# Halving the last down weights of each layer by columns, and issuing an even and an odd head's value products together

## What is computed

```python
for i in range(seq // BLOCK_Q):               # 128 queries at a time
    p = softmax(where(mask, q_i @ k[:q1].T * scale + bias, -inf))
    o_i = p @ v[:q1]                          # the value products
...
x = layer_norm(DN_ALPHA * x + mixer(x), *ln1)
x = layer_norm(DN_ALPHA * x + moe(x), *ln2)
...
def expert_step(acc, p):                      # over 64 experts
    wg, wu, wd, g = p                         # 1024x256, 1024x256, 256x1024
    hid = silu(t @ wg) * (t @ wu)
    return acc + (hid @ wd) * g[:, None], None
```

## Time and profile before

| what | value |
|---|---|
| median of 3 runs | 1332.64 us (1332.28 to 1334.15) |
| profiled execution | 1336.95 us |
| its span, first to last instruction | 1335.1 us |
| mean granted TensorE clock | 0.922 of full speed |
| PE busy | 1096.8 us (82%) |
| weight loads on PE | 658.8 us |
| VectorE busy | 414.9 us (31%) |
| ScalarE busy | 260.8 us (20%) |
| main DMA queue | 439.25 MB, 80.4% of the 16 engines' span |
| chain that ended last | PE 56%, DMA 35%, issue 3%, VectorE 2% |

### The profile page before, as it was taken

The page is one execution under the profiler, slowest core; times in us unless marked ns, Lnnn a source line. Parts: engine busy times, 40 slices in busy tenths (PEclk is TensorE's granted clock), DMA queues, the critical chain, the costliest instruction groups (busy, mean ns, idle before and its releaser), DMA issues.

```text
span 1335.1 us, 19927 instructions
## 1 busy us (share of the span) xinstructions
PE 1096.8 (82%) x7616; PEld 658.8 (49%) x7616; DVE 414.9 (31%) x993; ACT 260.8 (20%) x619; POOL 79.9 (6%) x106
## 2 busy tenths in 40 slices
PE   6988999999777766766599999999997776776664
PEld 4764754544444434433288866545544444333331
DVE  2584533332212222111322235433322122221113
ACT  3463322221111111111023223222111111111110
POOL 0443100000000000000240000000000000000000
PEclk9988899999988888888799999999999888888886
DMA  8172469999999999999951163599999999999993
GB/s 341 59 283 94 174 252 393 415 416 417 374 421 422 421 423 421 423 422 421 359 193 64 64 252 126 236 392 415 418 418 371 420 422 421 423 421 423 421 421 135
DMA packets 75745, 447.52 MB, mean 335 GB/s; under 512 B 7451, under 2 KB 20183, under 8 KB 25510
## 3 DMA queue, kind: packets, MB, share of 16 engines
q1 hardware_dynamic: 72640, 439.25, 80.4%
q0 software_dynamic: 1904, 6.46, 1.4%
q10 hardware_dynamic: 1142, 1.01, 0.2%
HBM read 445.61 MB, written 1.05 MB: 335 GB/s over the span
## 4 chain that ended last, share of the span: by engine, by line
PE 56%; DMA 35%; issue 3%; DVE 2%; SPq 2%; ACT 1%; ACTq 0%; DVEq 0%; POOL 0%; POOLq 0%
DMA ring<-in_l_exp_w_up 25%; PE bank L1002 11%; DMA ring<-in_l_exp_w_down 9%; PE bank L1127 8%; PE bank L1025 5%; PE bank L852 4%; PE bank L816 4%; PE bank L973 3%; PE bank L1105 3%; PE bank L918 2%; PE bank L1150 2%; PE bank L855 2%; PE bank L729 2%; SPq L579 2%; DMA mixT<-in_l_conv_w 1%
## 5 line engine op out<-in xcount | busy, mean ns | idle before, releaser
L1127 PE MATMUL bank<-ring,big 128*32 128x256 f32 x2816 | 217.0, 477 | 144.6 <-DMA ring<-in_l_exp_w_up 105.9
L1127 PEld LDWEIGHTS bank<-ring,big 128*32 128x32 f32 x2816 | 122.5, 136 | 233.7 <-issue 190.3
L1002 PE MATMUL bank<-ring,big 128*64 128x512 f32 x640 | 142.2, 596 | 0.0
L1873 DVE TENSOR_TENSOR big<-big,bank 128x256 f32<-128x256 f32 x22 | 9.3, 422 | 329.5 <-PE bank L1127 329.5
L1150 PE MATMUL bank<-ring,big 128*32 128x512 f32 x704 | 84.2, 620 | 15.8 <-DMA ring<-in_l_exp_w_down 15.5
L1892 DVE TENSOR_TENSOR mixT<-mixT,bank 128x512 f32<-128x512 f32 x128 | 84.0, 683 | 27.8 <-PE bank L1105 16.6
L1379 ACT ACTIVATE ys_high<-bank,gcol 128x512 fp32r<-128x512 f32 x84 | 57.7, 687 | 153.9 <-PE bank L1150 94.5
L1002 PEld LDWEIGHTS bank<-ring,big 128*64 128x64 f32 x640 | 44.0, 137 | 82.1 <-issue 80.5
L1037 PE MATMUL bank<-pick,xs_high 128*128 128x128 f32 x352 | 82.9, 280 | 0.0
L2001 POOL TENSOR_TENSOR rstd<-rstd,half 128x1 f32<-128x1 f32 x10 | 13.3, 1334 | 1145.9 <-DVE rstd L1467 1145.9
L1037 PE MATMUL bank<-pick,xs_low 128*128 128x128 f32 x352 | 81.0, 275 | 0.0
(11 more groups left out here) (287 smaller groups left out, 1400.1 us busy)
## 6 DMA issues: line engine op xcount, KB each, us to landing
ring<-in_l_exp_w_gate SPq DMA_DIRECT2D x128, 1024.0 KB, 16.8
ring<-in_l_exp_w_up SPq DMA_DIRECT2D x128, 1024.0 KB, 16.8
ring<-in_l_exp_w_down SPq DMA_DIRECT2D x128, 1024.0 KB, 18.4
ring<-in_l_w_in SPq DMA_DIRECT2D x12, 1024.0 KB, 12.3
ring<-in_l_w_out SPq DMA_DIRECT2D x8, 1024.0 KB, 6.0
ring<-in_l_w_in SPq DMA_DIRECT2D x4, 1440.0 KB, 15.2
par<-in_l_ln_g POOLq DMA_DIRECT2D x4, 512.0 KB, 6.4
par<-in_l_ln_b POOLq DMA_DIRECT2D x4, 512.0 KB, 7.4
```

The source lines that it names most:

```text
L1002: ins = mm(ps[SLOTS * q:SLOTS * q + SLOTS, :], xg[:, c, SLOTS * j:SLOTS * j + SLOTS], both[:, c], start=(c == 0), stop=(c == C - 1))
L1127: ins = mm(ps[r, 0:HID], xn[:, c, r], loop_weights(L, j, w)[:, c, :], start=(c == 0), stop=(c == C - 1))
```

## The change

It has two parts that do not touch each other.

- **Value products.** Nothing is issued for a head on its own. At each odd step from 3 on, ahead of the transposes of head h-1, the products of heads h-3 and h-2 are issued together: both heads' first matmul (256 columns), then both heads' second (128 columns). The even steps have no value products.
- **Last down weights.** In the last narrow group of each layer the four down tiles arrive as eight transfers of 512 KB: the left column halves of the four experts, then the right ones. A half row is 2 KB long, where a whole tile is 8 KB in one piece per partition. TensorE waits for the left halves alone, makes the left down products, scatters the left half of block 0, and only then waits for the right halves and makes the right down products. The other three scatters follow in the order 2, 1, 3. VectorE adds scatter 0 between the remainders of the two halves, and behind the branch 2, then 1, block 0's norm, then 3 and block 1's norm.

The semaphores `silu` and `high` are shared by the kinds of group, and `own_count` starts from the groups before; this makes room for `last_down0` and `last_down1`.

```diff
@@ plan_units
     u.loop(0, [((j, k), 3 * ((first[0] + j) % 4) + k) for j in range(GE) for k in range(3)], NGRP)
+    for j in range(GE):
+        u.n[u.at[(0, (j, 2))][0]] -= 1
@@ ExpertLoop
-        return self.S(f"{self.tag}_{self.kind}_{name}")
+        return self.S(f"{self.tag}_{name}")
...
+        return self.here(per, off + BEGIN[self.kind] * per * (2 if self.kind == "narrow" else 1))
@@ prog_sync
-                with sp.Fori(0, dict(KINDS)["narrow"] - 1) as i:
+                with sp.Fori(0, dict(KINDS)["narrow"] - 2) as i:
                     lp.i = i
                     refill(lp, in_place(lp.groups(GE, GE)))
+                lp.i = dict(KINDS)["narrow"] - 2
+                experts = in_place(lp.groups(GE, GE))
+                refill(lp, experts, BY_KIND[:2 * GE])
+                for h in range(2):
+                    part = slice(HALF * h, HALF * h + HALF)
+                    for j in range(GE):
+                        lp.read(sp, last_use_of_weights("narrow", j, 2))
+                        sp.dma_start(loop_weights(L, j, 2)[:, :, part], expert_weights(L, experts[j], 2)[:, :, part])\
+                          .then_inc(S(f"last_down{h}"), 16)
@@ prog_tensor, attention
+                    if h >= 3 and h % 2:
+                        key = ("ot", L, (h - 3) // 2)
+                        ps = bank_open(pe, key)
+                        for g in (h - 3, h - 2):
+                            bank_moved(pe, ("pt", L, g))
+                        if L == 1 and (h - 3) % 4 == 0:
+                            bank_moved(pe, ("v", (h - 3) // 4))
+                        for k, t, of in ((0, slice(0, T), slice(0, T)), (1, slice(P, T), slice(T, T + P))):
+                            for g in (h - 3, h - 2):
+                                r = slice(64 * (g % 2), 64 * (g % 2) + 64)
+                                ins = mm(ps[r, t], v[:, k, vd * g:vd * g + vd], pt[g % 2][:, of],
+                                         start=(k == 0), stop=(k == 1))
+                        bank_made(ins, key)
                     if 1 <= h <= heads:
                         g = h - 1
                         key = ("pt", L, g)
...
-                    if h >= 2:
-                        g = h - 2
-                        key = ("ot", L, g // 2)
-                        ps = bank_open(pe, key) if g % 2 == 0 else bank[banks.at[key][0]]
-                        bank_moved(pe, ("pt", L, g))
-                        if L == 1 and g % 4 == 0:
-                            bank_moved(pe, ("v", g // 4))
-                        r = slice(64 * (g % 2), 64 * (g % 2) + 64)
-                        mm(ps[r, 0:T], v[:, 0, vd * g:vd * g + vd], pt[g % 2][:, 0:T], start=True, stop=False)
-                        ins = mm(ps[r, P:T], v[:, 1, vd * g:vd * g + vd], pt[g % 2][:, T:T + P], start=False, stop=True)
-                        if g % 2:
-                            bank_made(ins, key)
@@ prog_tensor, narrow
-                    for j in range(GE):
-                        weights_landed(lp, j, 2)
-                    for h in range(2):
+                    if not last:
+                        for j in range(GE):
+                            weights_landed(lp, j, 2)
+
+                    def down(h):
+
+                        if last:
+                            pe.wait_ge(S(f"last_down{h}"), 16 * GE * (L + 1))
                         ps = lp.open(pe, ("dn", h))
...
+                    down(0)
+                    if last:
+                        pe.wait_ge(lp.sem("hot"), lp.count(1, 0, 1))
+                        scatter(0, 0)
+                        down(1)
+                        scatter(1, 0)
+                        scatter(0, 1)
+                        scatter(1, 1)
+                    else:
+                        down(1)
+                        pe.wait_ge(lp.sem("hot"), lp.count(1, 0, 1))
+                        for tb in range(TB):
+                            for h in range(2):
+                                scatter(tb, h)
@@ prog_vector, narrow
                         lp.done(ins, ("dn", h))
+                        if last and h == 0:
+                            add_rows(lp, 0)
@@ prog_vector, behind the branch
-                    for n in range(4):
+                    for n in (2, 1, 3):
                         add_rows(first_round, n)
...
+                    add_rows(first_round, 2)
                     for tb in range(TB):
-                        for h in range(2):
-                            add_rows(first_round, 2 * tb + h)
+                        add_rows(first_round, 2 * tb + 1)
```

More of the change, by code:

```diff
@@ L255, in own_count @@
     def own_count(self, per, off):
-        n = self.here(per, off)
-        return n if self.r is None else self.r * (NGRP * per) + n
+        if self.r is not None:
+            return self.r * (NGRP * per) + self.here(per, off)
+        return self.here(per, off + BEGIN[self.kind] * per * (2 if self.kind == "narrow" else 1))
     def at(self, key, back=0):
@@ L574, in prog_sync, with refill @@
                       .then_inc(S(f"unit_full{loop_unit(L, j, w)[0]}"), 16)
-                def refill(lp, experts):
-                    for j, w in BY_KIND if lp.kind == "narrow" else IN_ORDER:
+                def refill(lp, experts, pieces=None):
+                    for j, w in pieces or (BY_KIND if lp.kind == "narrow" else IN_ORDER):
                         lp.read(sp, last_use_of_weights(lp.kind, j, w))
@@ L1152, in narrow, with scatter @@
                         lp.made(ins, ("dn", h))
-                    pe.wait_ge(lp.sem("hot"), lp.count(1, 0, 1))
-                    for tb in range(TB):
-                        for h in range(2):
[L1157 to L1163, removed]
+                    def scatter(tb, h):
+                        lp.moved(pe, ("dn", h))
+                        ps = lp.open(pe, ("scatter", 2 * tb + h))
+                        for k in range(2):
+                            ins = mm(ps[:], hot[:, 0, P * tb:P * tb + P], ys[k][:, 0, HALF * h:HALF * h + HALF],
+                                     start=(k == 0), stop=(k == 1))
+                        lp.made(ins, ("scatter", 2 * tb + h))
+                    down(0)
[12 more added lines that the diff above has]
+                                scatter(tb, h)
                 pe.wait_ge(S("xs"), 2 * L + 2)
```

## The result

The changed kernel takes 1321.15 us in the median of 4 runs (1320.12 to 1321.53), against 1332.46 before: a ratio of 0.9915 with a 95% interval from 0.9895 to 0.9934, or 11.3 us less. Run again on another occasion it took 1320.27 us, ratio 0.9910 (0.9888 to 0.9931). The direction was right and the size was not: 11.3 us came where I had counted 7.35.

A forecast was written before the change was run, and what follows sets the result against it. TensorE bounds layer 1's attention without a gap, not layer 0's; narrow groups hang on the weights. Terms 3.45 + 1.6 + 0.6 + 1.7 = 7.35 us off 1332.64 give 1325.3 us, range 1321.8 to 1330.3.

The forecast's parts named there:

- Value products in layer 1: Layer 1's attention: paired heads overlap in part, 1.05 us a pair against 1.58; 3.45 us less (0.75 to 3.9).
- the last pair: End of layer 1's attention: both heads wait for ScalarE's copy, 2.18 us against 1.92, which takes 0.25 back.
- the staircase: Inside a value pair: eight short instructions start in issue order, same-strip passes following one another; 1.05 us a pair.
- the price of the turn: Layer 1's value products: turning from 64-column strips to something else costs 0.14 us, once a pair.
- Value products in layer 0: Layer 0's attention: pairs fill TensorE's idle time, ScalarE's delayed copy lies beside VectorE's convolution; 0, with 0.4 us either side.
- The tails: Last down products: left ones start at the hidden rows; 1.6 us gained in layer 1, 1.7 in layer 0.
- the additions: Layer 1's end: only one of VectorE's two additions remains ahead of block 1's norm; 0.6 us more gained.
- low-clock rival: Both tails: left products, pause and right products all at 1.2 GHz, -0.6 us a layer; 2.85 us in all, chance 0.12.
- No overlap: Layer 1's value products: short strips do not overlap, a pair saves only one turn, 0.75 us; total 4.65, chance 0.10.
- The branch holds layer 0's gain: Start of layer 1: the wait read as the taken branch does not move, layer 0's gain is nothing; 5.65 us, chance 0.10.
- The left halves are late: Both tails: left halves land with the right ones; 3.8 us lost in layer 1, 4.5 in layer 0; 1336.9, chance 0.04.

The follow-up runs named there:

- one_strip: The changed kernel with the odd head's products in the even head's 64 columns, head by head, and ScalarE copying each pair in two pieces; 1327.57 us, ratio 0.9977.
- head_by_head: The changed kernel with the even head's two matmuls issued first inside a pair, then the odd head's two; 1321.26 us, ratio 0.9920.
- before_again: The kernel before, unchanged, profiled once more; 1331.99 us, ratio 0.9989.
- pairs_layer1: The changed kernel with layer 0's value products as before, so pairs only in layer 1; 1321.55 us, ratio 0.9919.
- wait_all: The changed kernel with the left down products waiting for the right halves too; 1333.62 us, ratio 1.0023.

## Why the prediction was right and wrong

**Value products in layer 1: mechanism right, size wrong, and this is the step that failed.** The term was "Seven pairs inside the loop save 7 x (1.58 - 1.05) = 3.7 us (bounds 1.0 and 4.1)". Measured are 6.72 us for the whole attention and 0.37 that the last pair gives back, so 7.1 us, or 1.0 for each pair. Two errors went into it.

The larger one is the staircase. "Both passes of one matmul use the same strip, so they follow one another" is right (one_strip); what I made of it, that a waiting second pass also holds up the other strip's instructions issued behind it, is not. head_by_head refutes it: four instructions of one head ahead of the other cost nothing. The pair takes 0.81 us, and one_strip shows that without overlap it is 1.45.

The earlier trace rows could not have told me, and I misread it. The odd head's first product starts at 803.31 because ScalarE's copy of its probabilities ends only at 802.76 + 0.49 = 803.25, so the 0.10 us behind 803.21 is no lag at a change of strip. And its even neighbour's last pass starts at 803.32, where the staircase too would have let the odd head in. Timeline of before:

```profile
802.76 0.49 ACT L1222 ACTIVATE att<-bank 128x384 f32<-128x384 f32 x1
...
803.32 0.27 PE L690 MATMUL bank<-att,V 128*64 128x128 f32 x1
```

The row that decides stood in the same trace, at line 1002. Its matmuls alternate between the two strips, two passes each. By the staircase the second strip starts with the first one's second pass, 0.43 us behind. In a window of before around the first of them, of line 1002 alone, two instructions start within 0.01 us:

```profile
209.47:209.50 0.03, 0.01 (x2) 0.01 (x2) 1.00 0.00 0
```

I had read only the mean of these 64, 0.217 us, which both models give, and so made my own model the upper bound. The rule of the Trainium skill that I stayed below (TensorEngine Tiling (Array Packing), Theoretical Speedup: up to 2x for 64 columns) fits the trace: 1.58 us to 0.81.

The smaller one is the price of the turn. Of the 1.03 us between two steps of before_again and of after, 1.60 - 0.81 = 0.79 lie in the pair. The other 0.24 lie in the neighbours, which I had left alone: behind a 64-column product the first score matmul takes 774.15 - 773.83 = 0.32 us to the next one, behind a transpose 769.46 - 769.24 = 0.22, and from the transposes to the value products it is 0.42 against 0.33 to 0.38 to the scores. Some 0.09 go back where the output projection now stands ahead of the pair.

The last pair gives back 0.37 (the stretch from the last transposes is 792.17 - 789.88 = 2.29 us, 1.92 before); I had 0.25. That this came out near is two errors that cancel: the wait for ScalarE's copy grew from 1.13 to 1.49 us, since both heads are now transposed one behind the other and ScalarE first copies the first head's probabilities and the pair before, and the pair takes 0.80 and not 1.05. That the shift is carried to the end holds: TensorE's way from the attention to the first expert group is 37.3 us in eleven of the twelve traces, the exception being before_again.

**Value products in layer 0: counted 0 (0.4 to either side), measured 0.7 us lost.** TensorE did have idle time. What I priced at nothing was ScalarE's later copy, which "lies beside VectorE's convolution". The order of the steps alone makes VectorE's 60 instructions 3 to 22 ns longer on average. That VectorE's convolution is slower beside GpSimd's additions, and that the two overlap more in the new order, the traces show (pairs_layer1). What makes them overlap more is only argued: GpSimd's waits for ScalarE are 11.5 to 12.2 us in the four traces with the old order and 12.2 to 13.6 in the eight, so a later ScalarE fits.

**The tails: mechanism right, and both near the favourable end.** The middle values were 1.6 us in layer 1 and 1.7 in layer 0, with 2.8 and 2.5 as the ends at the upper clock; measured against before are 2.49 and 2.46, against before_again 1.90 and 2.51, and 0.6 for the additions, exactly as counted. What I halved was the clock's part. In all eight traces with an early left product the 16 left instructions take 1.92 us, the duration of the upper clock, and the one kernel that lets TensorE stand for 4.7 to 5.0 us first (wait_all) shows 0.52 to 0.54. The whole tiles, with 2.7 and 3.2 us of standing in before_again, show 0.56 and 0.68. So the low-clock rival had too much chance: I noted that the left products fill the idle stretch, and then took the middle all the same. The rule of the Trainium skill that I cited for this rival (TensorE: Matmul & The Clock Gate, Part 1: throttled by default, released by activity) agrees with these traces; it speaks for the change, since the idle time goes.

**The other rivals.** *No overlap* is refuted by one_strip, which is what it would have looked like. *The branch holds layer 0's gain*: refuted, the first transposes come 10.64 us behind the last down product, 10.35 before, so 2.2 of the 2.5 us are carried; the 0.3 that go back I had not counted. *The left halves are late*: it did not happen, but wait_all confirms the mechanism. Over whole stages it costs 4.1 us in each layer against before, in layer 1 with the 0.6 of the additions already won, so 4.1 and 4.7 in layers 0 and 1, where I had 4.5 and 3.8. The size of the whole was right.

**The sum** with measured terms: 6.7 + 2.5 + 2.5 + 0.6 - 0.7 - 0.3 = 11.3 us, where the time shows 11.3 and 12.2; that the first agrees to the tenth is luck, since the interval of the first is 2.6 us to either side. Against the 7.35 forecast, 3.3 us more came from the value products of layer 1 and 1.65 from the clock in the tails. The range failed because its lower end was built on an upper bound of the overlap (3.9 us for the attention, where 6.7 came) that was a model of mine and no row.

## What to carry to other kernels

Matmuls that use half of the array's columns are worth pairing even when they are short: in this shape two such streams of four instructions took the time of one, whatever their order, and two changes of strip width fewer saved another 0.39 us, partly in the neighbours. At a stage that waits for its last weights, let the first half of the work start on half of the transfer; here the early work saved its own time, and the clock stayed up for what followed. When you compare such tails, count from an event that both kernels wait for: counted from the hidden rows, wait_all looked 2.4 us worse than it was. When an upper bound comes from your own model of the issue order, look in the trace for one row that the model forbids before you use it; single starts tell what a mean does not.

## What the runs showed of the hardware

Products in two different 64-column strips do not hold each other up in the order of issue: 0.81 us a pair in both orders, 1.45 in one strip. Pieces of 2 KB went at 385 GB/s beside 8 KB at 426 and 1 KB at 348, near the line through the two (388). VectorE's 128x256 multiply-adds took 478 to 481 ns alone and 821 to 860 ns where GpSimd's additions overlapped them. Reordering TensorE's work in layer 0 made their mean longer (623 to 628 ns to 631 to 647), though VectorE waited for TensorE only once there, 2.0 us in either order.
